# A gather of 256 expert rows that feeds three engines: TensorE's second wait per row, the place of the second query, single weights for the last eight rows, and the last norm by halves

## The reference

```python
def peer_ffn(h, w_q, sub_keys, u, v):            # PEER_HEADS 8, TOPK 16, 128 x 128 experts
    def block(xb):                               # 128 tokens
        q = (xb @ w_q).reshape(n, PEER_HEADS, 2, PEER_HALF)
        s = jnp.einsum('nhpc,hpkc->nhpk', q, sub_keys)
        s_top, i_top = lax.top_k(s, PEER_TOPK)
        cand_s = (s_top[:, :, 0, :, None] + s_top[:, :, 1, None, :]).reshape(n, PEER_HEADS, -1)
        ...
        best_s, best_pos = lax.top_k(cand_s, PEER_TOPK)
        ids = jnp.take_along_axis(cand_i, best_pos, axis=-1)
        gate = jax.nn.softmax(best_s, axis=-1)
        act = jax.nn.gelu(jnp.einsum('nd,nhkd->nhk', xb, u[ids]), approximate=False)
        return jnp.einsum('nhk,nhkd->nd', gate * act, v[ids])
...
x = x + peer_ffn(rms_norm_2(x, g_ffn), ...)
return rms_norm_2(x, g_final)
```

## Time and profile before

| | us |
|---|---|
| median of three runs | 2127.94 |
| the three runs | 2125.16, 2127.94, 2135.51 |
| the profiled execution's own time | 2135.83 |
| its span, first to last instruction | 2134.1 |
| gather stage: first row requested, last output issued | 1461.12, 2131.04 |
| mean of the granted TensorE clock | 0.974 |

### The profile page before, as it was taken

How to read it: one execution, slowest core, us unless ns; L and a number is a source line. 1 busy time by engine, 2 the same in 40 slices (tenths; PEclk the granted TensorE clock), 3 DMA queues, 4 the chain that set the end, 5 groups by cost and what they waited for, 6 DMA issues and landing times.

```text
span 2134.1 us, 20902 instructions
## 1 busy us (share of the span) xinstructions
PE 1939.1 (91%) x7920; PEld 1423.8 (67%) x7920; DVE 1052.3 (49%) x2563; ACT 497.0 (23%) x1205; POOL 319.6 (15%) x332
## 2 busy tenths in 40 slices
PE   4999899999999999999999999998887878887877
PEld 4876688888887788888889777786443433433333
DVE  6993466501597432000210323225767767767754
ACT  2123321101113322110100544312223223222223
POOL 1000001100000000000000000002444434444442
PEclk9999999999999999999999999999999999999899
DMA  9711079944351133448652222435999999999997
GB/s 401 289 59 60 21 314 371 397 161 155 139 199 68 73 144 141 153 154 179 249 183 80 109 79 79 188 128 235 401 422 422 421 421 409 421 421 421 421 422 291
DMA packets 71715, 517.38 MB, mean 242 GB/s; under 512 B 8128, under 2 KB 8384, under 8 KB 11456
## 3 DMA queue, kind: packets, MB, share of 16 engines
q0 software_dynamic: 46384, 330.85, 38.9%
q1 hardware_dynamic: 25232, 185.21, 22.9%
HBM read 510.78 MB, written 5.24 MB: 242 GB/s over the span
## 4 chain that ended last, share of the span: by engine, by line
PE 72%; DMA 15%; DVE 9%; ACT 3%; issue 1%; SPq 0%; another core or an unknown queue 0%; POOL 0%; DVEq 0%; ACTq 0%
PE pj L579 17%; DMA region<-in_peer_uv,small 12%; PE pj L784 9%; PE pj L799 9%; PE st L1052 8%; PE pj L731 5%; DVE region L1941 3%; PE pj L592 3%; PE pj L1021 2%; PE pj L623 1%; PE pj L828 1%; PE st L866 1%; PE pj L925 1%; DMA pe_T<-in_pe_cols 1%; DMA ring<-in_ring_w 1%
## 5 line engine op out<-in xcount | busy, mean ns | idle before, releaser
L1052 PE MATMUL st<-region 128*128 128x512 f32 x940 | 446.5, 627 | 113.1 <-ACT region L1402 112.9
L1052 PEld LDWEIGHTS st<-region 128*128 128x128 f32 x940 | 180.2, 198 | 371.7 <-issue 196.0
L579 PE MATMUL pj<-hT,ring 128*128 128x256 f32 x1760 | 384.1, 380 | 1.0 <-ACT region L1228 1.0
L579 PEld LDWEIGHTS pj<-hT,ring 128*128 128x128 f32 x1760 | 333.6, 190 | 47.4 <-ACT region L1228 1.8
L1941 DVE CUSTOM_DVE_ANT_0 region<-region 128x1024 f32<-128x1024 f32 x235 | 285.5, 1223 | 116.5 <-DMA region<-in_peer_uv,small 114.5
L497 POOL DMA_INDIRECT region<-in_peer_uv,small x235 | 256.3, 1091 | 398.1 <-PE st L1052 328.4
L784 PE MATMUL pj<-region,ring 128*128 128x256 f32 x1024 | 222.2, 379 | 4.1 <-ACT region L1228 2.7
L784 PEld LDWEIGHTS pj<-region,ring 128*128 128x128 f32 x1024 | 194.2, 190 | 32.4 <-ACT region L1228 3.5
L1560 DVE SCALAR_TENSOR_TENSOR region<-region,pc 128x255 f32<-128x255 f32 (+19 forms) x528 | 202.7, 467 | 0.0
L1512 DVE TENSOR_TENSOR tmp<-xT,hT 128x256 f32<-128x256 f32 x32 | 13.6, 425 | 366.4 <-ACT hT L1129 366.4
L1402 ACT ACTIVATE region<-ident,small 128x128 f32<-128x128 f32 x256 | 89.0, 394 | 377.5 <-DVE small L1949 377.5
(11 more groups left out here) (345 smaller groups left out, 2020.1 us busy)
## 6 DMA issues: line engine op xcount, KB each, us to landing
ring<-in_ring_w SPq DMA_DIRECT2D x157, 1024.0 KB, 4.9
region<-in_ada_rest POOLq DMA_DIRECT2D x40, 1024.0 KB, 12.4
region<-in_ada_first SPq DMA_DIRECT2D x4, 2048.0 KB, 17.6
region<-in_wqkv SPq DMA_DIRECT2D x2, 3072.0 KB, 12.3
region<-in_wcmp POOLq DMA_DIRECT2D x2, 2048.0 KB, 9.4
bias_dram<-region POOLq DMA_DIRECT2D x1, 4096.0 KB, 46.9
region<-in_w_o POOLq DMA_DIRECT2D x4, 1024.0 KB, 6.2
region<-in_peer_uv,small POOLq DMA_INDIRECT x235, 15.8
```

Source lines behind the costliest of these rows:

```text
L579: i = nc.tensor.matmul(b[:, m, :], w[:, k, P * m:P * m + P], hT[:, k, :], start=(k == 0), stop=(k == CT - 1))
L1052: i = nc.tensor.matmul(acc[:, u % 2, 512 * hf:512 * hf + 512], diag[:, m % NDIAG, :], uv[m % NBUF][:, D + 512 * hf:D + 512 * hf + 512], st ...
```

## The change

Four edits, all in the gather stage and behind it.

1. TensorE no longer waits for `uv_row` ahead of each slot's products, only for `diag_ready`.
2. Head 1's query on TensorE moves from ahead of row 0 to behind row 3, its sub-scores from behind row 1 to behind row 5. ScalarE's copies move with them: the query's behind the second pair of diagonals, the scores' behind the third. VectorE's retrieval of unit 2 moves from the dots of rows 9, 11, 13 to those of rows 10, 12, 14.
3. The last eight slots are weighed singly, where it was the last four.
4. Token tile 1's final norm is done by halves of 512 columns: the first half is squared as soon as the last slot's first half is summed (a new semaphore, `half_summed`), its sum passes through a small ScalarE step (Identity with a scale and a bias) and becomes the bias of the root; VectorE scales the tile in two pieces and SyncE writes it in two.

```diff
-SINGLES = SLOTS - 4
+SINGLES = SLOTS - 8
...
-            for s in range(2):
-                sp.wait_ge(sem("out_ready"), s + 1)
-                sp.dma_start(out[0, P * s:P * s + P, :], h_tok[:, s, :]).then_inc(sem("out_done"), 16)
-            sp.wait_ge(sem("out_done"), 32)
+            for n, (s, lo, hi) in enumerate(((0, 0, D), (1, 0, 512), (1, 512, D))):
+                sp.wait_ge(sem("out_ready"), n + 1)
+                sp.dma_start(out[0, P * s:P * s + P, lo:hi], h_tok[:, s, lo:hi]).then_inc(sem("out_done"), 16)
+            sp.wait_ge(sem("out_done"), 48)
...
-            peer_query(1)
             for m in range(2 * PH * TOPK):
...
                 pe.wait_ge(sem("diag_ready"), m + 1)
-                pe.wait_ge(sem(f"uv_row{m % NBUF}"), 16 * (m // NBUF + 1))
                 for hf in range(2):
                     i = nc.tensor.matmul(acc[:, u % 2, 512 * hf:512 * hf + 512], ...)
+                    if m == SLOTS - 1 and hf == 0:
+                        i.then_inc(sem("half_summed"), 1)
                 i.then_inc(sem("v_used"), 1)
-                if m == BATCH - 1:
+                if m == 2 * BATCH - 1:
+                    peer_query(1)
+                elif m == 3 * BATCH - 1:
                     sub_scores(1)
...
-                    if g == 0:
+                    if g == 1:
                         keep_query(1)
+                    elif g == 2:
                         keep_scores(1)
...
-            final_std(1)
+            act.wait_ge(sem("out_ready"), 1)
+            act.wait_ge(sem("half_summed"), 1)
+            link(nc.scalar.activation(h_tok[:, 1, 0:512], acc[:, 1, 0:512], ACT.Square, accum_out=mstat[:, 0, 0:1]))
+            link(nc.scalar.activation(mstat[:, 1, 0:1], mstat[:, 0, 0:1], ACT.Identity, bias=eps_col[:, 0:1], scale=1.0 / D))
+            act.wait_ge(sem("v_used"), SLOTS)
+            link(nc.scalar.activation(h_tok[:, 1, 512:D], acc[:, 1, 512:D], ACT.Square, accum_out=mstat[:, 0, 1:2]))
+            nc.scalar.activation(mstat[:, 1, 1:2], mstat[:, 0, 1:2], ACT.Sqrt, bias=mstat[:, 1, 0:1], scale=1.0 / D).then_inc(sem("last_std"), 1)
...
-                nc.vector.scalar_tensor_tensor(h_tok[:, s, :], acc[:, s, :], mstat[:, 1, s:s + 1], g_fin, ALU.mult, ALU.mult).then_inc(sem("out_ready"), 1)
+                for lo, hi in ((0, D),) if s == 0 else ((0, 512), (512, D)):
+                    nc.vector.scalar_tensor_tensor(h_tok[:, s, lo:hi], acc[:, s, lo:hi], mstat[:, 1, s:s + 1], g_fin[:, lo:hi], ALU.mult, ALU.mult).then_inc(sem("out_ready"), 1)
...
-                tops, pairs, numbers = (9, 11, 13) if n < TOPK else (3, 7, 11)
+                tops, pairs, numbers = (10, 12, 14) if n < TOPK else (3, 7, 11)
```

## The result

| | before | changed |
|---|---|---|
| median, us | 2129.82 | 2138.30 |
| runs | 20, 2125.16 to 2135.51 | 20, 2132.07 to 2144.36 |
| ratio, 95% interval | | 1.0036 [1.0026, 1.0047] |
| profiled execution, own time and span | 2135.83, 2134.1 | 2133.45, 2131.7 |

What follows compares the result with a forecast made beforehand. The prediction took DMA, with one late engine ending the rows, as the bound; +5.0 - 0.8 - 1.2 = +3.0 us, so a median of 2130.9 us from 2127.94, range 2122 to 2138.

Steps and rivals of the forecast that it cites:

- The query's move, +5.0: First rows of the gather stage: moving head 1's query delays weighings and row requests, +5.0 us, bounds -2.4 to +7.
- Row 22's lateness costs 1 us per us: Row 22's request had no slack, so it and all rows behind it land 5.0 us later.
- The dry queue as evidence: Rows near 20 and 22: queue nearly dry, a request needing at least 7.9 us to land; 2.4 us lost before.
- The wait taken out, -0.8: TensorE in the gather stage: 256 instructions less save about one fetch of 11, -0.8 us, bounds 0 to -1.5.
- Eight singles, -0.45: Stage's end: weighing singly from slot 248 clears TensorE's backlog, so row 254 starts when its diagonal is made, -0.45 us.
- Halves, -0.75: Token tile 1's final norm and output: -0.15 us on the norm and -0.6 us on the smaller last write.
- The savings in sum, -2.0: Gather stage and end: -0.8 us from the wait and -1.2 us from singles and halves together.
- Cover for the lateness: Rival, first rows: early requests keep the queue fed, the old 2.4 us loss stays; -2.0 us, 2125.9 us, 22%.
- healing of the old hole: Rival, DMA gap from row 20: the early buffer release closes it too; -4.4 us, 2123.5 us, 10%.
- Lateness carried through the later queries: Rival, heads 3 to 7: each of five query blocks loses 2.4 us, +12, with the rest 2142.9 us; 6%.
- TensorE as the bound: Rival, gather stage: TensorE bounds and each removed wait cost 0.05 us; 13 us faster, 2115 us, 5%.
- The signs of being wrong: Forecast fails if row 22 is requested before 1523 us, or row 255 lands no later than before.

Runs made afterwards that it cites:

- e7: Changed kernel with head 1's query, sub-scores, copies and unit 2's retrieval back in their old places; ratio to the kernel before 0.9995 [0.9987, 1.0004].
- e12: e7 with eleven row buffers in place of twelve; ratio to the kernel before 1.0003 [0.9993, 1.0012].
- e9: Changed kernel with 11 filler products of the identity added on TensorE behind row 1; ratio to the kernel before 1.0025 [1.0013, 1.0037].
- e2: Kernel before with only head 1's query moved behind row 3, its sub-scores, copies and unit 2's retrieval with it; ratio to before 1.0025 [1.0012, 1.0037].
- e5: Changed kernel with TensorE's wait for uv_row put back; ratio to the kernel before 1.0031 [1.0016, 1.0045].
- e11: Changed kernel run once more, unaltered, for a second profile; a single run of 2142.29 us.
- e6: Changed kernel with ScalarE's copies of head 1's query and scores one pair later; ratio to the kernel before 1.0013 [1.0002, 1.0023].
- e3: Kernel before with only the last eight slots weighed singly; ratio to the kernel before 1.0004 [0.9994, 1.0014].
- e4: Kernel before with only token tile 1's norm and output by halves; ratio to the kernel before 1.0000 [0.9987, 1.0013].
- e1: Kernel before with only TensorE's wait for uv_row taken out; ratio to the kernel before 1.0004 [0.9994, 1.0013].
- e10: e7 with head 1's query behind row 1 and its sub-scores behind row 3, retrieval in its old place; ratio to before 1.0001 [0.9989, 1.0012].

## Why the prediction was right or wrong

What it said: no change by the 0.5% bound, +3.0 us, with +5.0 from the moved query against -2.0 of savings. What came: +7.7 us [5.5, 10.0], so no change by that bound. The sign and the cause hold; the query's term is too small, and of the savings less showed in e7. The hit is a near one. Added to the three runs' 2127.94 the measured change gives 2135.6 us, inside the 2122 to 2138 of the forecast; the median that was measured, 2138.30, lies just above. The bounds of the terms alone ended at +7.5 us, and the 2.6 us added for scatter made the room.

- **What bounds the stage**: right, it is DMA. A share of about one engine in sixteen ends the rows in the changed kernel too, and a shorter ring whose requests stay early enough moved nothing (e12). That a q8 fetch is what makes the last engine late is shown by no run.
- **The query's move, +5.0**: mechanism right, too small. The chain stands in the profiles at its places: the weighing of rows 4 and 5 came 2.3 us later in the first profile (36.6 us behind the first request), 2.6 with the filler (e9) and 4.6 to 6.0 in e2, e5 and e11 (38.9 to 40.3; forecast 38.4), row 22 at 63.8 and 68.8 (forecast 65.3). Alone it cost 5.3 us [2.6, 7.9] (e2), in company 8.7 (e7 against the changed kernel). Two things are seen to add to it. The clock: I charged 1.1 us; on rows 2 and 3 it was 0 in one profile of the changed kernel and 2.8 us in the other (e11), and 1.7, 2.7 and 2.9 us in e2, e5 and e6. There are more falls later in the same rows: in the 32 us of the hole the mean clock is 0.95 in e2, e5, e6 and e11, and 1.00 in the others. And the reference: the profile that I read had row 22 at 60.3 us and a hole of 2.6 us, while e3, e4 and e7, with the same order over these rows, had it at 56.0 to 58.8 and little or none. In it and in e1 head 1's query took 8.13 and 8.76 us, in e3 and e4 7.07. With the sub-scores ahead of it (1.19 us before, 0.68 in e3) that makes the 1.5 and 1.7 us by which row 22 is later in these two than in e3 and e4, and in e7 the early copy gives 2.8 us more. So the move starts from a lower base. What the later retrieval of unit 2 adds can be read between the requests of rows 20 and 22: 5.9 us in the changed kernel and e9, 5.3 with the old places (before, e3, e4, e7, e10), 0.5 us where the prediction had 0.4. In every run with the moved query but e10 it moved too, and it was not timed by itself.
- **Row 22's lateness costs 1 us per us**: right behind a threshold. Over the fourteen profiles the stage stays at 657.2 to 658.3 us for requests up to 58.8 us, is 660.1 to 661.9 for 60.3 to 63.8, 663.2 and 664.7 at 64.1 and 64.6, and 666.9 to 667.4 for 67.5 to 68.8. I had put the threshold at the profile's own 60.3. The DMA rates give the same account. The loss against 421 GB/s in the hole is 0 to 8.7 us, and in e2, e5 and e11 about 2 us more are lost in the 33 us ahead of it (394 to 397 GB/s). In every profile the stage is longer than e7's by that loss, within 1.4 us.
- **The dry queue as evidence**: the prediction weighed its rivals by 7.9 us as the least time to land (it did allow for less in its bounds) and took the hole for a fixed trait of the kernel. Row 0's 5.5 us in the same profile, and e3, e4 and e7, show neither.
- **The wait taken out, -0.8**: the fetch goes, as said (10 packets in all eight profiles without the wait and without filler; 11 in the five with it, and in e9, whose filler adds 22 rows of its own). Of its price, -0.8 us, the runs show nothing: +0.8 us [-1.3, +2.8] in e1.
- **Eight singles, -0.45**: 12.04 to 11.60 us behind the last dot; the product starts at once on row 254's diagonal. Right in size in the profile, too small for the medians to show.
- **Halves, -0.75**: -0.62 in e4's profile. The write gave its 0.6; in the changed kernel the norm took 2.94 us from TensorE's end to the last scaling's end, against 2.98 before, so the 0.15 was mostly not there. The prediction's 2.8 us was a slip: its own terms, with root and inverse at the 0.30 and 0.16 us of the profiles, add up to 2.95.
- **The savings in sum, -2.0**: e7 measured -1.1 us [-2.8, +0.9], so neither -2.0 nor nothing is excluded.
- **The rivals.** Cover for the lateness, and healing of the old hole: not so in any profile with the move behind row 3; in part so in e10. Lateness carried through the later queries: no, the changed kernel's DMA is back at 421 GB/s between 1900 and 2000 us. TensorE as the bound: e1 excludes its 13 us.
- **The signs of being wrong**: both came about in absolute time. Row 22 was requested before 1523 us (1522.65), and row 255's dot was not later than before (2120.72 against 2122.02), only because the stage began 2.3 us earlier. Counted from the first request row 22 was 3.5 us late and the last dot 1.0. The signs had to be put relative to the stage's start.

Open: why the first request moves by 13 us between profiles; what holds ScalarE's copy until 14.2 us in some of them; and how much of the difference between 5.3 and 8.7 us is scatter of the medians. The clock's share was not isolated by timing (e9's interval overlaps).

## What to carry to other kernels

A piece of work that stands early in an engine's hand-written order may be there because nothing else can run then: head 1's query ran while VectorE still retrieved unit 1, and behind row 3 it lay on the path of the buffers that follow. Before moving it, find the deadline on the queue that bounds the stage (here row 22's request, between 58.8 and 60.3 us after the first) and how far the old order is from it, in more than one profile. An idle time opened on TensorE can cost more than its length, since the work behind it may run on the lower clock, as in e11 and not in the first profile.

## What the runs showed of the hardware

- The same program had eight 128x512 products in 3.70 us in one execution and in 6.49 in another, behind idle times of 3.43 and 3.25 us; the granted clock was 1.00 and 0.50. The Trainium skill, "TensorE: Matmul & The Clock Gate" (Part 1), says that the number of products that run at the lower clock varies from run to run; the rows of e11 and of the changed kernel agree. Here the slower products delay the row requests behind them, and the stage is 667.4 us long in the one and 661.9 in the other.
- Instruction fetches of 16 KB stand among the queues of the DMA engines that carry the data: 256 waits less were one packet less of eleven, in all the profiles but e9's.
- A 1 MB indirect row request with nothing ahead of it in the queue (row 0) landed in 5.6 us (e7); in the profile of before VectorE starts on row 0 after 5.5 us.
